# A hybrid conv/GLA decoder step on one core: value tiles moved into the conv turns, cg tiles moved into seven-product couples

## What is computed

```python
h = rmsnorm(x, norm_pre1) * (1 + sc1) + sh1
proj = h @ w_in    # bg, cg, ua | q, k, v, r, lr | ga, gb
y_a = bg * causal_dwconv(cg * ua, ...)             # branch A, width 3
log_a = log_sigmoid(lr @ w_a2 + b_a) / 16          # per token and key channel
# branch B: S_t = diag(exp(log_a_t)) S_{t-1} + k_t^T v_t ; o_t = q_t S_t
merged = sigmoid(ga) * y_a + sigmoid(gb) * (rmsnorm(o) * silu(r))
x = x + g1 * rmsnorm(merged @ w_out)
a, gt = split(h2 @ w_up) ; x = x + g2 * rmsnorm((gelu(causal_dwconv(a)) * gt) @ w_down)
```

## Time and profile before

| | us |
|---|---|
| median of 3 runs | 968.18 (968.15 to 970.20) |
| the profiled execution, its whole time | 968.57 |
| its span, first to last instruction | 966.8 |
| PE busy in the span | 945.3 (98%) |
| DVE, ACT, POOL busy | 623.0, 458.1, 170.1 |

### The profile page before, as it was taken

The page is one execution under the profiler, slowest core; times in us unless marked ns, Lnnn a source line. Parts: engine busy times, 40 slices in busy tenths (PEclk is TensorE's granted clock), DMA queues, the critical chain, the costliest instruction groups (busy, mean ns, idle before and its releaser), DMA issues.

```text
span 966.8 us, 18387 instructions
## 1 busy us (share of the span) xinstructions
PE 945.3 (98%) x7479; PEld 858.8 (89%) x7479; DVE 623.0 (64%) x924; ACT 458.1 (47%) x771; POOL 170.1 (18%) x101
## 2 busy tenths in 40 slices
PE   5999999999999998999999999999999999999997
PEld 4889999888888897999998799999999999888886
DVE  2687777401787876535538689999998998660204
ACT  4565455534343343452553356566555566534112
POOL 3010000443233333323353000000000000012430
PEclk9999999999999999999999999999999999999999
DMA  9754844758676669438336041233333332312212
GB/s 327 252 76 95 110 94 88 177 141 69 157 225 153 217 180 103 112 82 171 119 109 213 1 131 45 75 101 88 91 107 88 107 91 73 124 66 87 87 52 98
DMA packets 133508, 115.57 MB, mean 120 GB/s; under 512 B 9945, under 2 KB 110065, under 8 KB 133425
## 3 DMA queue, kind: packets, MB, share of 16 engines
q1 hardware_dynamic: 133329, 114.37, 46.9%
q10 hardware_dynamic: 96, 0.04, 0.0%
HBM read 107.02 MB, written 7.35 MB: 118 GB/s over the span
## 4 chain that ended last, share of the span: by engine, by line
PE 93%; DVE 3%; ACT 2%; issue 1%; DMA 1%; POOL 0%; SPq 0%; DVEq 0%; ACTq 0%; POOLq 0%
PE pair L2519 31%; PE pair L2426 26%; PE pair L2594 17%; PE pair L2868 5%; PE pair L2416 2%; PE pair L2649 1%; PE pair L2676 1%; PE pair L2356 1%; DMA x_tok<-in_x_prompt 1%; PE pair L2586 1%; PE pair L2730 1%; PE pair L2741 1%; PE pair L2587 1%; PE pair L2588 1%; PE pair L2585 1%
## 5 line engine op out<-in xcount | busy, mean ns | idle before, releaser
L988 POOL TENSOR_TENSOR w_lo<-raw,w_hi 128x1024 fp32r<-128x1024 f32 x41 | 102.6, 2504 | 610.7 <-ACT w_hi L1063 494.5
L2426 PE MATMUL pair<-h_hi,w_hi 128*128 128x288 f32 x624 | 144.8, 305 | 0.6 <-POOL w_lo L992 0.5
L2426 PE MATMUL pair<-h_lo,w_hi 128*128 128x288 f32 x624 | 138.5, 295 | 0.5 <-issue 0.5
L2426 PE MATMUL pair<-h_hi,w_lo 128*128 128x288 f32 x624 | 138.9, 296 | 0.0
L2426 PEld LDWEIGHTS pair<-h_hi,w_hi 128*128 128x128 f32 x624 | 101.6, 188 | 11.5 <-issue 8.8
L2519 PE MATMUL pair<-h_hi,w_hi 128*128 128x288 f32 x348 | 102.8, 295 | 0.0
L1063 ACT ACTIVATE w_hi<-raw 128x1024 fp32r<-128x1024 f32 x54 | 57.0, 1057 | 96.5 <-PE pair L2588 80.2
L2426 PEld LDWEIGHTS pair<-h_hi,w_lo 128*128 128x128 f32 x624 | 102.0, 188 | 0.7 <-issue 0.6
L2519 PE MATMUL pair<-h_hi,w_lo 128*128 128x288 f32 x348 | 102.4, 294 | 0.0
L2519 PE MATMUL pair<-h_lo,w_hi 128*128 128x288 f32 x348 | 102.3, 294 | 0.0
L2426 PEld LDWEIGHTS pair<-h_lo,w_hi 128*128 128x128 f32 x624 | 101.8, 188 | 0.0
(11 more groups left out here) (397 smaller groups left out, 2114.7 us busy)
## 6 DMA issues: line engine op xcount, KB each, us to landing
raw_c<-in_w_ada SPq DMA_DIRECT2D x32, 512.0 KB, 5.7
raw<-in_w_in SPq DMA_DIRECT2D x96, 128.0 KB, 3.5
raw<-in_w_up SPq DMA_DIRECT2D x24, 512.0 KB, 3.8
raw<-in_w_down SPq DMA_DIRECT2D x22, 512.0 KB, 3.7
raw_up<-in_w_up SPq DMA_DIRECT2D x20, 512.0 KB, 3.8
ada_first<-in_w_ada SPq DMA_DIRECT2D x16, 512.0 KB, 9.8
raw_c<-in_w_in SPq DMA_DIRECT2D x128, 64.0 KB, 4.3
raw<-in_w_in SPq DMA_DIRECT2D x128, 64.0 KB, 3.4
```

The costliest lines, as they stand in the source:

```text
L988: pool.tensor_tensor(lo, raw_tile(n)[:, :], hi.bitcast(F32), ALU.subtract).then_inc(S("w_lo_done"), 1)
L2426: ins = pe.matmul(bank[pair][:, half, 0:HALF], w[:, i, :], x[:, i, HALF * half:HALF * half + HALF], start=i == 0 and p == 0, stop=i == KT ...
```

## The change

Three things are moved, and what is computed stays the same.

- **cg as couples.** The eight cg tiles become four more couples (couples 10 to 13, `GATES_END` = 10). Their sums go to two buffers in turn, `cg_out0` and `cg_out1`, which share memory with `raw_c0`/`raw_c1` and `raw_c4` of the adaLN loads; ACT evicts the last quarter (`cg_last`). Each finished couple is stored to HBM (`store_cg`, 128x2x576, 590 KB, one store after another) and each channel tile is loaded again for its turn (`load_cg`, 295 KB, `buf_a` and `buf_b` in turn).
- **Value tiles in the turns.** The stretch of eight 512-column value tiles is gone. Each turn has, in place of the cg tile, one value tile of 512 contraction rows by 256 columns (`value_tile`): 4 blocks x 4 token tiles x 3 = 48 matmuls of 256 columns, and 4 x 2 for the samples. Two turns make 256 columns of v (one head); ACT evicts them in the odd turns (`values_out`) and DVE adds the sample halves (`values_sum`). `h_smp_hl` holds only half of the contraction now, and ACT fills it again in each turn (`stack_samples`, two operations of 128x256). PSUM pair 0 takes the u tile of every turn, where three pairs took turns before.
- **Decay logs at the head of the first turn.** ACT makes them between the last couple and its own first-turn work, and DVE's subtraction and the clearing of `suf` stand behind the item of slot 2 of the first turn.

The diff, without the renumbering of landing counts, the merged semaphore `own_made`, and the waits of the head turns:

```diff
...
-EARLY = HEADS // 2 + KT
-TILE_K, TILE_E, TILE_V = 0, HEADS, HEADS + 4 * EARLY
-TILE_C1 = TILE_V + 8
+GATES_END = HEADS // 2 + KT
+EARLY = GATES_END + KT // 2
+TILE_K, TILE_E = 0, HEADS
+TILE_C1 = TILE_E + 4 * EARLY
...
             def load_c1(n):
-                i = n - TILE_C1
-                load_raw(n, in_cols((IN_CG, IN_UA)[i % 2] + P * (i // 2)))
+                j, x = divmod(n - TILE_C1, 2)
+                if x:
+                    load_raw(n, in_cols(IN_UA + P * j))
+                else:
+                    cols = IN_V + DV * (j // 2)
+                    load_raw(n, w_in[512 * (j % 2):512 * (j % 2) + 512, cols:cols + DV].rearrange("(k p) c -> p k c", p=P))
+
+            def store_cg(m):
+                c = GATES_END + m
+                sp.wait_ge(S("c_sum"), 3 * c + 3)
+                sp.wait_ge(S("cg_done"), m + 1)
+                if m > 0:
+                    sp.wait_ge(S("cg_stored"), 16 * m)
+                sp.dma_start(cg_kept[2 * m:2 * m + 2, :, :].rearrange("a p t -> p a t"), cg_out[m % 2][:, :, :]) \
+                  .then_inc(S("cg_stored"), 16)
+
+            def load_cg(j):
+                if j % 2 == 0 and j < 4:
+                    sp.wait_ge(S("cg_stored"), 16 * (j // 2 + 1))
+                if j > 0:
+                    sp.wait_ge(S("cg_in"), 16 * j)
+                if j > 1:
+                    sp.wait_ge(S("u_done"), 3 * (j - 1))
+                sp.dma_start((buf_a, buf_b)[j % 2][:, :], cg_kept[j, :, :]).then_inc(S("cg_in"), 16)
...
+            store_cg(0)
+            load_c1(TILE_C1)
+            load_c1(TILE_C1 + 1)
+            store_cg(1)
+            load_cg(0)
             load_c1(TILE_C1 + 2)
...
+            load_c1(TILE_C1 + 3)
+            store_cg(2)
+            store_cg(3)
+            load_cg(1)
+            sp.wait_ge(S("ya_done"), YA_E)
+            sp.wait_ge(S("ring_free"), TILE_C1)
+            sp.wait_ge(S("cg_stored"), 16 * (KT // 2))
+            for x in range(4):
+                load_ada(x)
...
             for i in range(4, 2 * KT + 4, 2):
                 for r in (i, i + 1):
                     if r < 2 * KT:
                         load_c1(TILE_C1 + r)
                     else:
                         load_c2(r - 2 * KT)
+                if 6 <= i < 2 * KT + 2:
+                    load_cg(i // 2 - 1)
                 if i >= 6:
                     for x in range(2 * i - 8, 2 * i - 4):
                         load_ada(x)
...
+            def cg_last(c):
+                m = c - GATES_END
+                act.wait_ge(S("ring_free"), early_product(c, 6))
+                if m > 1:
+                    act.wait_ge(S("cg_stored"), 16 * (m - 1))
+                act.activation(cg_out[m % 2][:, 1, 0:HALF], one_bank(2 + c % 2)[:, 0:HALF], ACT.Copy).then_inc(S("cg_done"), 1)
...
+                else:
+                    high(TILE_C1 + 2)
+                    cg_last(c)
+
+            def stack_samples(kh):
+                for src, cols in ((h_hi, slice(0, 64)), (h_lo, slice(64, P))):
+                    act.activation(h_smp_hl[:, :, cols], src[:, 4 * kh:4 * kh + 4, SEQ:T].bitcast(F32), ACT.Copy) \
+                       .then_inc(S("stacked"), 1)
+
             act.wait_ge(S("h_lo_done"), KT)
-            act.activation(h_smp_hl[:, :, 0:64], h_hi[:, :, SEQ:T].bitcast(F32), ACT.Copy).then_inc(S("stacked"), 1)
-            act.activation(h_smp_hl[:, :, 64:P], h_lo[:, :, SEQ:T].bitcast(F32), ACT.Copy).then_inc(S("stacked"), 1)
-            high(TILE_V + 2)
+            stack_samples(0)
...
+            def values_out(b):
+                cols = slice(DV * b, DV * b + DV)
+                act.wait_ge(S("ring_free"), TILE_C1 + 4 * b + 3)
+                for x in range(2):
+                    src = one_bank(V_BANK + x).rearrange("p (t c) -> p t c", c=DV)
+                    act.activation(v_tok[:, 2 * x:2 * x + 2, cols], src, ACT.Copy).then_inc(S("v_done"), 1)
+                src = one_bank(V_BANK + 2)
+                act.activation(v_tok[0:64, NCH, cols], src[64:P, 0:DV], ACT.Copy).then_inc(S("v_done"), 1)
+                act.activation(v_tok[64:P, NCH, cols], src[0:64, 0:DV], ACT.Copy).then_inc(S("v_done"), 1)
...
                 high(n + 3)
                 mix_history(j)
-                act.wait_ge(S("ring_free"), n + 1)
-                if j > 0:
-                    act.wait_ge(S("u_done"), 3 * j)
-                act.activation(halves(buf_a[:, :]), out2(c1_pair(j, 0)), ACT.Copy).then_inc(S("cg_done"), 1)
+                if j % 2:
+                    values_out(j // 2)
+                if j + 1 < KT:
+                    act.wait_ge(S("ring_free"), n + 1)
+                    stack_samples((j + 1) % 2)
                 high(n + 4)
                 if j + 1 < KT:
                     qd_exp(act, j + 1)
...
+            dve.wait_ge(S("ring_free"), TILE_C1)
...
-            dve.wait_ge(S("z_abs"), 6)
-            dve.wait_ge(S("z_min"), 4)
-            dve.tensor_tensor(pre[:, :, :], pre[:, :, :], suf[:, :, :], ALU.subtract).then_inc(S("z_min"), 1)
-            dve.wait_ge(S("z_min"), 5)
-            dve.memset(suf[:, :, :], 0.0).then_inc(S("level_set"), 1)
...
+            def values_sum(b):
+                v_smp = v_tok[:, NCH, DV * b:DV * b + DV]
+                dve.wait_ge(S("v_done"), 4 * (b + 1))
+                dve.tensor_tensor(v_smp, v_smp, one_bank(V_BANK + 2)[:, 0:DV], ALU.add).then_inc(S("v_summed"), 1)
...
+                dve.wait_ge(S("cg_in"), 16 * (j + 1))
...
+                for src, dst, lo, hi in conv_pieces(0, ext, 2, TS + 2, 2):
+                    dve.tensor_tensor(dst, src, piece((buf_a, buf_b)[j % 2], lo, hi), ALU.mult).then_inc(S("u_done"), 1)
...
+                    if j == 0 and e == 2:
+                        dve.wait_ge(S("z_abs"), 6)
+                        dve.wait_ge(S("z_min"), 4)
+                        dve.tensor_tensor(pre[:, :, :], pre[:, :, :], suf[:, :, :], ALU.subtract).then_inc(S("z_min"), 1)
+                        dve.wait_ge(S("z_min"), 5)
+                        dve.memset(suf[:, :, :], 0.0).then_inc(S("level_set"), 1)
+                if j % 2:
+                    values_sum(j // 2)
                 if j + 1 < KT:
                     level_queries(dve, j + 1)
...
-                    ins = token_tiles(TILE_V + n, n % 4, V_BANK[c], h_hi, h_lo, n % 4 == 0, n % 4 == 3, "v_mm", tiles, h_smp_hl)
...
+            def value_tile(n, kh, part):
...
+                for t in ((0, 1), (2, 3, NCH))[part]:
+                    dst = one_bank(V_BANK + t // 2)[:, DV * (t % 2):DV * (t % 2) + DV]
+                    for i in range(4):
+                        first, last = kh == 0 and i == 0, kh == 1 and i == 3
+                        if t == NCH:
+                            both = h_smp_hl[:, i, :]
+                            ins = pe.matmul(dst, both, wh[:, i, :], start=first, stop=last, skip_group_check=True)
+                            ins = pe.matmul(dst[0:64, :], both[:, 0:64], wl[:, i, :], start=False, stop=last,
+                                            skip_group_check=True)
+                            continue
+                        xh, xl = (x[:, 4 * kh + i, P * t:P * t + P] for x in (h_hi, h_lo))
+                        for p, (x, w) in enumerate(((xh, wh), (xh, wl), (xl, wh))):
+                            ins = pe.matmul(dst, x, w[:, i, :], start=first and p == 0 and t % 2 == 0, stop=last and p == 2,
...
-                        channel_tile(kc(w_hi[n % 4]), kc(w_lo[n % 4]), c1_pair(j, x), (h_hi, h_lo), part=e % 4 // 2)
+                    n = TILE_C1 + 2 * j + e // 4
+                    if e in (0, 4):
+                        pe.wait_ge(S("w_lo_done"), n + 1)
+                    if e in (0, 2):
+                        if j == 0:
+                            pe.wait_ge(S("cg_done"), KT // 2 - 1 + e // 2)
+                            pe.wait_ge(S("c_sum"), 3 * EARLY)
+                        elif j % 2 == 0:
+                            pe.wait_ge(S("v_done"), 2 * j)
+                            if e == 2:
+                                pe.wait_ge(S("v_summed"), j // 2)
+                        if e == 2:
+                            pe.wait_ge(S("stacked"), 2 * (j + 1))
+                        value_tile(n, j % 2, e // 2)
+                    elif e in (4, 6):
+                        if e == 4 and j > 0:
+                            pe.wait_ge(S("u_done"), 3 * j)
+                        channel_tile(kc(w_hi[n % 4]), kc(w_lo[n % 4]), 0, (h_hi, h_lo), part=e // 2 - 2)
...
```

141 lines of the change are left out of this document (45 added, 96 removed).

## The result

The changed kernel is slower: 973.33 us, median of 6 runs (970.65 to 975.26), against 968.63 of the kernel before on the same chip; ratio 1.0047 [1.0032, 1.0061]. The forecast was 968.0 with a range up to 973.3, so the median lies just beyond the range's end, on the side that had 0.31. The profiled execution took 974.99 us, at the upper end of its runs; its span is 6.4 us longer than that of before.

What follows compares the result with a forecast made beforehand. PE, busy in 98% of the span, was taken as the bound. Matmuls -4.0 and a first-turn wait +3.6 gave -0.4 us: 968.2 from the profiled 968.57, 967.8 as median, plus 0.2 for an unnamed wait: 968.0, range 964.3 to 973.3.

Steps and rivals of the forecast that it cites:

- the side that had 0.31: Whole kernel: the outcome slower, given a chance of 0.31, against 0.40 for the same and 0.29 for faster.
- Matmuls: PE: value stretch out -51.07 us, four couples in +44.7, value tiles for cg tiles +2.4; sum -4.0 us.
- Both rivals on the spacing: Value tiles' matmuls: 106 ns apart, 962.7 us, chance 6%; or 0.133 us as at 288 columns, 973.3 us, 13%.
- Decay logs, the second chain: First turn: DVE done with the logs at T + 13.5; they alone would leave 0.9 us of PE wait.
- T: The start of the first turn on PE, from which the prediction counts its times in us.
- Stores: Last cg stores of 590 KB: 3.2 us each from issue to landing, the fourth landing at T + 3.8.
- That rival: Slower by the stores: at 5 us each the first turn's wait is 6.8 us, 971.2 us; chance 12%.
- Landing of C1+4: First turn: C1+4, fifth in the load queue, lands at T + 13.8; PE waits 3.6 us at its fifth item.
- The clock ... I expect it to stay: Whole kernel: the clock stays at 1.00, the upper level of 2.4 GHz, with no time added for it.
- The rest, at nothing: Couples 10 to 13 and the turns: other work of DVE, ACT and SP adds no time; `rows_ada` wait stays 2.6 us.
- 0.5 us of "issue": PE in the kernel before: a wait for nothing the trace names; 0.2 us added for another of its kind.
- the first turn is not held: First turn: C1+4 isn't late, only the decay logs' 0.9 us of wait stay; 965.3 us, chance 20%.

Runs made afterwards that it cites:

- stall: Kernel before, with DVE clearing the conv buffer 12 times ahead of `conv_input(0)` so that PE waits at the first turn's last item: 978.27 us, ratio 1.0097.
- filler: Changed kernel, with 40 matmuls of 288 columns that nothing reads on PE ahead of the first turn's last item: 972.56 us, ratio 1.0039.
- load_first: Changed kernel, with the load of C1+4 asked for between the third and fourth cg store, not behind the adaLN loads: 971.57 us, ratio 1.0028.
- exp_first: Changed kernel, with ACT in the first turn taking the next level's exponential ahead of the rounding of C1+4: 971.49 us, ratio 1.0021.
- order_logs: Changed kernel, with SP's stores and loads reordered (C1+4 earlier) and the decay logs moved into couples 11 to 13: 973.23 us, ratio 1.0046.
- tuned: order_logs, with the second turn's adaLN loads ahead of C1+6 and C1+7, and C1+7's pieces asked for in pairs: 977.29 us, ratio 1.0084.
- extra: Kernel before, with 12 more 64 KB pieces of block 3's columns copied to an unread HBM buffer behind the fifth turn's adaLN loads: 969.88 us, ratio 1.0003.
- ada_first: tuned, with adaLN loads ahead of the weight tiles in all turns and C1+9's pieces in pairs too: 972.99 us, ratio 1.0043.
- other_cols: order_logs, with tile C1+7 reading block 2's columns instead of block 3's, same byte counts: 969.82 us, ratio 1.0001.
- light_loads: load_first, with the 16 adaLN loads of turns 2 to 5 bringing half of their rows: 971.96 us, ratio 1.0031.
- best_keep: best, with 17 matmuls that nothing reads in place of PE's 2.6 us wait for `rows_ada` after the last turn: 968.17 us, ratio 0.9986.
- best: ada_first, with ACT rounding tile n+4 behind the next level's two exponentials in all turns but the last: 969.60 us, ratio 1.0001.
- late_keep: best_keep, with the rounding of tile n+4 moved further back, behind `mix_tails(j)`: 966.62 us, ratio 0.9976.
- tuned_keep: tuned, with 17 matmuls that nothing reads where PE would wait 2.6 us for `rows_ada` after the last turn: 976.36 us, ratio 1.0072.

## Why the prediction was wrong, point by point

- *Matmuls.* Right. Couples 10 to 13 ended within 0.3 us of their place (four times 11.17 us, no wait), value matmuls 120 ns apart against 119.4, turns 0.3 us longer. Both rivals on the spacing are out. (288 and 512 columns lie 13 and 15 ns above their stream, not 11 to 13; nothing hangs on it.)
- *Decay logs, the second chain.* Right in place and size: DVE done at T + 13.6 (13.5), 0.7 and 1.3 us of wait where they alone were left (0.9), nothing won by moving them alone.
- *Stores.* 2.9 and 3.3 us against 3.2; landed at T + 3.95 against T + 3.8. That rival is out.
- *Landing of C1+4.* The step that was mis-sized: 11.8 us after the first adaLN issue and not 9.3 to 10.5, since I took four loads at 1.4 us each, and here two came 2.9 us apart and C1+5's pieces shared the last. The wait was 5.3 and not 3.6 us, outside 3.0 to 4.2 and inside the bounds.
- *"The clock ... I expect it to stay, since a wait of a few us is all that the change can add in one place."* The step that failed: it left the clock out of the sum. Behind the 5.3 us wait the granted clock was 0.5 for 6.8 us, and again for 3.4 us behind `rows_ada`. That cost 3.7 us in the profiled execution and some 2 in stall. With it the forecast would have been some 970 to 972. Of the 6.5 us between the forecast's sum (-0.4) and the measured one (+6.1) it is the largest part; the wait has 1.7, the pause of 0.9 most of the rest. What part the clock has in the median is not shown, as filler says.
- *The rest, at nothing.* Failed in one place: PE's program blocks come over the same DMA engines as the data, and the 51 us of value stretch, under which the loads of the first turns used to run, are gone. The slow loads of block 3 were in the earlier trace rows, 0.92 at 59 GB/s, and I passed over them. The earlier trace rows had 0.5 us of "issue" that I left unnamed and priced at 0.2.
- *Rival "the first turn is not held", 965.3 us.* Its condition was made in load_first, exp_first and order_logs, and gave 971.5 to 973.2. The price was wrong since something else takes the wait's place. By the traces it is the late block, 0.4 us of pause with the wait and up to 4.7 without; that the wait had covered for it is argued, not shown.

## What to carry to other kernels

When work is removed under which loads used to run, sum the bytes that now have to come in the stretch behind it, and look at the lowest rate in it, not the mean; here PE stood still at one place or another as long as loads that it needed late were asked for, or taken by ACT, ahead of what it needed soon. An engine that takes its work in order must not take a tile for two turns later ahead of what the present turn waits for. Price a new wait of several us on TensorE with the slower matmuls behind it, and name every "issue" row of before, however small.

## What the runs showed of the hardware

- The 20 profiled executions have 29 stops of PE put to "issue" between 178 and 400 us. 26 of them, 0.3 to 4.7 us, ended 2.25 to 2.8 us after a 16 KB packet of the instruction queue began. The other three, 1.5 to 2.8 us, stand at adaLN products, 3.0 to 5.4 us after one; two of these products had their weights 1.4 us before. In the turns of the kernel before 3.7 to 12.0 us pass between two such packets; it was 14.3 in order_logs and 18.6 in tuned, ahead of the pauses of 4.1 and 4.7. 13.0 in extra and 14.2 in ada_first had no pause or one of 0.5.
- Eight pieces of 64 KB that differ in nothing but the columns that they read took 8.1 us from first to last landing (block 3, order_logs) and 6.7 us (block 2, other_cols), with a median of 147 and 27 ns for the 512-byte packets meanwhile; all DMA traffic of the stretch ran at 74 GB/s at a share of 1.05, and at 151 GB/s at 0.73. Copied within HBM in extra, columns of block 3 were slow as well, 58 GB/s at 1.04 while the first six pieces ran. Why, stays open.
- In the profiled executions the clock fell in or behind waits of 1.8, 2.0, 2.6, 4.1, 4.2, 4.7, 5.3, 5.5 and 6.9 us, and behind two of 1.5 and 1.6 us in a row (exp_first). It stayed at waits of 1.6, 1.8, 1.9 and 2.1 us in light_loads, best_keep, best and late_keep. Behind the one of 2.6 us it fell in eleven kernels and stayed in six, before among them. With 17 matmuls in that wait it stayed in best_keep, tuned_keep and late_keep.
